# Strip input rows at a stride of 576 elements, split weights 128 bytes further on, a smaller dynamic scratch

## The chip, the cores and the metric

The kernel runs on one core of one Trainium2 chip. The metric is the device time of one execution in microseconds. Engines are called PE (TensorE; PEld is its weight load), ACT (ScalarE), DVE (VectorE), POOL (GpSimd) and SP (SyncE, which issues DMAs).

## What is computed

Two transformer layers in a row on 512 tokens of width 1024, in float32, each behind 16 meta tokens, so that 528 positions are worked on. The first layer merges three branches (a chunkwise retention, a differential attention, a short convolution) and has an MLP of 4096 with a squared ReLU. The second merges a stick-breaking attention and a gated linear attention and has a gated MLP of 2816 with a short convolution. Nearly all arithmetic is in the products of activations with weight matrices:

```python
(rq, rk, rv, rg, dq, dk, dv, cb, cc, cx, gates) = [h @ w_in[:, s:e] for s, e in column_bounds()]
merged = g0 * (ret @ w_branch[0]) + g1 * (diff @ w_branch[1]) + g2 * (conv @ w_branch[2])
x = x + merged @ w_out
x = x + jnp.square(jax.nn.relu(rms_norm(x, norm2_w) @ w_up)) @ w_down
# second layer
proj = hn @ w_in_2
mix = (gate_sb * (sb @ w_sb_out) + gate_gla * (o @ w_gla_out)) @ w_o
ffn = (gelu(causal_dwconv(hn @ w_ffn_up)) * (hn @ w_ffn_gate)) @ w_ffn_down
```

## The kernel before

Activations lie feature-major: a buffer `[128, 8, 528]` has feature 128 c + p in row c of partition p, and 528 columns, one for each position (T = 528, HALF = 264, NM = 16, SEQ = 512). A weight matrix is cut into strips of 128 output features: `[128, 8, 128]`, eight blocks of 128 by 128, 512 bytes each in a partition.

*Three products for one.* Products are made in the format fp32r, from a high and a low part of each operand. `xh` and `xl` (or `bh` and `bl`) hold the parts of the activations, `wh` and `wl` those of the weights, and a strip is wh x hi + wh x lo + wl x hi, added up in PSUM.

*The pipeline of a strip.* SP loads strip n into `wraw` (two slots, 512 KB each, line 466). ACT copies it to `wh` (`split_hi`, from line 548, the copy is line 553), DVE subtracts to get `wl` (`split_lo`, the subtraction is line 1231), PE multiplies (`strip`, from line 2150, its matmul is line 2171), DVE or ACT reads PSUM. ACT may split strip n + 1 only when PE is through with strip n - 1 (`mm_done`). There are 299 such loads by SP.

*The order within a strip.* As a rule a strip is three passes: all eight rows with wh and hi, all eight with wh and lo, all eight with wl and hi. If all 528 positions are wanted, a row is two matmuls of 264 columns, one after the other, with the same weights (16 in a pass); if only the 512 tokens are, it is one of 512 columns that begins at column 16 (8 in a pass). A strip whose input rows are still being made (`ready` is given) goes row by row in place of that: the three products of row 0, then those of row 1, and so on. Every matmul has its own load of weights.

*Other users of these buffers.* Line 2770 (`chunk_products`) makes the down product of the second MLP with tokens as output partitions: there 512 columns of wh or wl are the moving operand and 128 columns of a bh or bl row, from column 16 + 128 t on, the stationary one. Line 2294 (`st_product`) makes blocks of 256 tokens with additions of sub-blocks in place of some multiplications, from xh, xl and other buffers. In the stick-breaking attention, which needs only four rows of xh and xl, the upper four (`sb_hi`, `sum_hi`) serve as flat scratch. POOL loads the 12 tables of decays and slopes into `hf` one head ahead (line 2877), the only transfers whose descriptors software makes.

*Placement.* Buffers are laid out in the order in which they are allocated, behind the scratch for dynamic transfers (16384 bytes in a partition) and 128 bytes of constants: xh, xl, bh, bl, wraw, wh, wl, then all the others.

Of the kernel before, what the change touches and what calls it, by code (L numbers as in the profile page):

```python
# [21 lines left out]
F32R = mybir.dt.float32r  # L22
# [5 lines left out]
P = 128  # L28
D = 1024
KC = D // P  # L30
NM = 16
SEQ = 512
T = NM + SEQ
# [4 lines left out]
DH, DHD = 8, 64  # L38
LAM_INIT = 0.2
FF1 = 4 * D  # L40

SH, SHD = 8, 64
GH, GDV = 4, 256
# [37 lines left out]
def flat(ap):  # L81
    return ap.rearrange("p a t -> p (a t)")
# [35 lines left out]
def build(nc, weights, cols, tables, consts, lam_rows, post_rows, x_t, meta2_t, wgk, gla_masks, res_dram,  # L118
          mrg_dram, tx_dram, out):
    ctx = ExitStack()  # L120
    with ctx:
        def sb(name, shape, dt=F32):
            return ctx.enter_context(nc.sbuf_tensor(name, shape, dt))
# [4 lines left out]
        def shared(name, shape):  # L128

            with nc.sbuf_tensor(name, shape, F32) as plain:  # L130
                pass
            return plain, sb(name + "_r", shape, F32R)


        xh, xl = sb("xh", [P, KC, T], F32R), sb("xl", [P, KC, T], F32R)
        bh, bl = sb("bh", [P, KC, T], F32R), sb("bl", [P, KC, T], F32R)

        wraw = sb("wraw", [P, 2, KC, P])
        wh, wl = sb("wh", [P, 2, KC, P], F32R), sb("wl", [P, 2, KC, P], F32R)
        qq, qqr = shared("qq", [P, KC, T])  # L140
        kk, kkr = shared("kk", [P, KC, T])
        vt, vtr = shared("vt", [P, 5, D])
# [44 lines left out]
        SBW = SBA + SBB + SBC  # L187
# [3 lines left out]
        sbr = [flat(kkr)[:, SBW * e:SBW * e + SBW] for e in range(2)]  # L191
        SBZ = 272 + 400 + 400
        sums = [[flat(r)[:, SBZ * e:SBZ * e + SBZ] for e in range(2)] for r in (xrows, xrowsr)]
        sb_hi = [flat(r[:, 4:8, :])[:, 0:SBW] for r in (xh, xl)]
        sum_hi = [flat(r[:, 4:8, :])[:, SBW:SBW + 672] for r in (xh, xl)]
        sum2_hi = [gater[:, 144 * e:144 * e + 144] for e in range(2)]
        ntri_r, nones_r = hfr[:, 1, 0:P], hfr[:, 1, P:2 * P]
        sb_v = tmp[:, 0, :]
# [2856 lines left out]
```

How the kernel before makes its waits and increments, by code:

```python
    def __call__(self, ins):  # L91
        ins.then_inc(self.sem, 1)
        self.n += 1
        self.eng.wait_ge(self.sem, self.base + self.n)
# [368 lines left out]
        @block.sync  # L463
# [5 lines left out]
            def strip_pairs(first, end):  # L469
                if first < end:
                    with sp.Fori(first, end) as i:
                        for k in range(2):
                            sp.wait_ge(lo_done, 2 * i + k - 1)
                            load(2 * i + k, k)
# [9 lines left out]
                    sp.dma_start(st_area(q)[:, 2 * k:2 * k + 2, :].rearrange("p b n -> p (b n)"),  # L484
                                 weights[n0 + k].rearrange("p k n -> p (k n)")).then_inc(st_in[q % 2][k], 16)
            gates = gate_pairs()
            strip_pairs(1, 9)
            load_area(*gates[0])
            strip_pairs(9, 12)
            for m, (q, n0) in enumerate(gates):
                if m + 1 < CONV_PAIRS:
                    sp.wait_ge(*((lo_done, n0 - 2) if m else (t_made, 4)))
                    load_area(*gates[m + 1])
                for k in range(2):
                    sp.wait_ge(lo_done, n0 - 1 + k)
                    load(n0 + 2 + k, k)
            gates = gate_pairs("ret")
            strip_pairs(START["ret_qkv"] // 2, gates[0][1] // 2)
            sp.wait_ge(op_ready, 2 * KC)
            for m, (q, n0) in enumerate(gates):
                if m == 0:
                    load_area(*gates[0])
# [118 lines left out]
            def st_copy(q, src, dst, product, k):  # L623
                act.wait_ge(st_mm, 5 * q + product)
                if k == 0:
```

## Time and profile before

| | |
|---|---|
| median of 3 runs | 2125.64 us (2125.48 to 2125.77) |
| the profiled execution, first to last instruction | 2123.7 us |
| PE busy | 2111.8 us (99%), 13662 matmuls |
| PEld busy | 1859.1 us (88%) |
| DVE busy | 1241.8 us (58%) |
| ACT busy | 831.0 us (39%) |
| POOL busy | 165.7 us (8%) |
| DMA, mean over the span | 96 GB/s |

The profile gives no own run time of the profiled execution; its span is 1.9 us below the median. Busy time counts overlapping matmuls once. The duration of one matmul is from its start to its modelled end, and successive ones overlap; the time from one start to the next is called its pace here.

### The profile page before, as it was taken

The numbers are of one execution on the slowest core, as the hardware profiler recorded it, in microseconds if no ns is written. First come the engines' busy times: TensorE is split into PE (matmuls) and PEld (weight loads), VectorE is DVE, ScalarE is ACT, GpSimd is POOL, SyncE is SP. The second block draws the span as 40 slices with busy tenths as digits, with TensorE's granted clock in tenths as the row PEclk, the third lists the DMA queues.
The fourth block names the chain that finished last, engine by engine and source line by source line (L and its number), as shares of the span: only waits on it lengthen the run. The fifth ranks groups of instructions, "written<-read, shape, count | busy, mean of one in ns | idle before, by whom it ended". The sixth has DMA issues, their size and how long they took to land.

```text
span 2123.7 us, 33898 instructions
## 1 busy us (share of the span) xinstructions
PE 2111.8 (99%) x13662; PEld 1859.1 (88%) x13662; DVE 1241.8 (58%) x1847; ACT 831.0 (39%) x1305; POOL 165.7 (8%) x146
## 2 busy tenths in 40 slices
PE   9999999999999999999999999999999999999998
PEld 8998888788888788898898888999999998889897
DVE  6674444564555555767664666367855567446364
ACT  4333222433444443434434566343424344222233
POOL 0012000030000000232120000022300000000000
PEclk9999999999999999999999999999999999999999
DMA  4343221522222323332322221231133222322322
GB/s 149 109 171 107 85 75 60 198 81 82 73 68 68 106 94 98 107 109 80 109 90 90 88 91 50 90 121 54 58 136 106 90 79 90 99 90 89 99 90 99
DMA packets 53563, 203.36 MB, mean 96 GB/s; under 512 B 6960, under 2 KB 7344, under 8 KB 52288
## 3 DMA queue, kind: packets, MB, share of 16 engines
q1 hardware_dynamic: 49248, 177.56, 26.1%
q10 hardware_dynamic: 3232, 20.80, 2.5%
q0 software_dynamic: 960, 3.24, 0.5%
q8 instruction: 91, 1.49, 0.3%
q14 instruction: 32, 0.26, 0.0%
HBM read 190.96 MB, written 10.62 MB: 95 GB/s over the span
## 4 chain that ended last, share of the span: by engine, by line
PE 94%; DVE 3%; ACT 2%; issue 0%; DMA 0%; DVEq 0%; SPq 0%; ACTq 0%
PE ps L2171 70%; PE ps L2294 7%; PE ps L2770 6%; PE ps L2636 1%; PE ps L2418 1%; PE ps L2443 1%; PE ps L2371 1%; PE ps L2702 1%; PE ps L2542 1%; DVE kk_r L1824 1%; PE ps L2457 1%; ACT kk L963 1%; ACT kk L964 1%; PE ps L2680 0%; PE ps L2523 0%; PE ps L2350 0%
## 5 line engine op out<-in xcount | busy, mean ns | idle before, releaser
L553 ACT ACTIVATE wh<-wraw 128x1024 fp32r<-128x1024 f32 x284 | 300.0, 1056 | 747.6 <-PE ps L2171 632.1
L1231 DVE TENSOR_TENSOR wl<-wraw,wh 128x1024 fp32r<-128x1024 f32 x298 | 366.9, 1232 | 135.8 <-ACT wh L553 131.7
L2171 PE MATMUL ps<-xh,wh 128*128 128x264 f32 (+1 forms) x1800 | 327.6, 327 | 0.5 <-DVE tmp L1264 0.4
L2171 PE MATMUL ps<-xl,wh 128*128 128x264 f32 (+1 forms) x1800 | 321.3, 324 | 0.0
L2171 PE MATMUL ps<-xh,wl 128*128 128x264 f32 (+1 forms) x1800 | 320.8, 323 | 0.0
L2171 PEld LDWEIGHTS ps<-xh,wh 128*128 128x128 f32 x1800 | 264.7, 188 | 31.6 <-issue 2.4
L2171 PEld LDWEIGHTS ps<-xl,wh 128*128 128x128 f32 x1800 | 266.2, 188 | 28.6
L2171 PEld LDWEIGHTS ps<-xh,wl 128*128 128x128 f32 x1800 | 266.1, 188 | 28.4
L2171 PE MATMUL ps<-bh,wh 128*128 128x264 f32 (+1 forms) x1296 | 234.4, 325 | 0.2 <-ACT wh L553 0.2
L2171 PE MATMUL ps<-bl,wh 128*128 128x264 f32 (+1 forms) x1296 | 231.0, 322 | 0.0
L2171 PE MATMUL ps<-bh,wl 128*128 128x264 f32 (+1 forms) x1296 | 230.6, 322 | 0.0
L2171 PEld LDWEIGHTS ps<-bh,wh 128*128 128x128 f32 x1296 | 190.9, 188 | 21.7 <-issue 1.5
L2171 PEld LDWEIGHTS ps<-bl,wh 128*128 128x128 f32 x1296 | 191.3, 188 | 19.8 <-issue 0.2
L2171 PEld LDWEIGHTS ps<-bh,wl 128*128 128x128 f32 x1296 | 191.0, 188 | 19.6
L1264 DVE TENSOR_TENSOR qq<-ps,rsq 128x528 f32<-128x528 f32 (+1 forms) x44 | 30.8, 700 | 98.3 <-PE ps L2171 98.2
L1264 DVE TENSOR_TENSOR tmp<-ps,rsq 128x528 f32<-128x528 f32 x31 | 21.9, 707 | 81.2 <-PE ps L2171 79.2
L561 ACT ACTIVATE bh<-hf 128x512 fp32r<-128x512 f32 (+1 forms) x30 | 19.0, 632 | 88.4 <-DVE hf L2079 51.4
L2770 PE MATMUL ps<-wh,bh 128*128 128x512 f32 x176 | 50.1, 393 | 0.3 <-ACT ps L1199 0.3
L2770 PE MATMUL ps<-wh,bl 128*128 128x512 f32 x176 | 50.0, 393 | 0.0
L2770 PE MATMUL ps<-wl,bh 128*128 128x512 f32 x176 | 50.0, 393 | 0.0
L2917 POOL TENSOR_TENSOR qq<-qq,kk 128x512 f32<-128x512 f32 x3 | 5.0, 1663 | 571.8 <-DVE qq L2139 571.8
L1724 DVE SCALAR_TENSOR_TENSOR hf<-ps,rsq 128x512 f32<-128x512 f32 x32 | 22.1, 689 | 38.2 <-PE ps L2171 38.2
(532 smaller groups left out, 2779.6 us busy)
## 6 DMA issues: line engine op xcount, KB each, us to landing
wraw<-weights_dram SPq DMA_DIRECT2D x299, 512.0 KB, 3.5
qq<-weights_dram SPq DMA_DIRECT2D x12, 512.0 KB, 4.1
kk<-weights_dram SPq DMA_DIRECT2D x12, 512.0 KB, 4.4
hf<-tables_dram POOLq DMA_DIRECT2D x12, 264.0 KB, 3.0
res<-x_t_dram SPq DMA_DIRECT2D x4, 528.0 KB, 7.1
res<-x_t_dram ACTq DMA_DIRECT2D x1, 2112.0 KB, 9.2
res_dram<-res ACTq DMA_DIRECT2D x1, 2112.0 KB, 6.4
mrg_dram<-mrg ACTq DMA_DIRECT2D x1, 2112.0 KB, 9.0
```

What stands on the lines that cost most here:

```text
L553: nc.scalar.activation(wh[:, slot], wraw[:, slot], ACT.Copy).then_inc(hi_done, 1)
L963: link(nc.scalar.activation(sbt[e], sbt[e], ACT.Exp, scale=-1.0))
L964: nc.scalar.activation(sbt[e], sbt[e], ACT.Ln, bias=1.0).then_inc(slog_done, 1)
L1231: nc.vector.tensor_tensor(wl[:, slot], wraw[:, slot], wh[:, slot].bitcast(F32), ALU.subtract)\
L1264: return nc.vector.tensor_tensor(dst, src, row(rsq, n), ALU.mult)
L1724: nc.vector.scalar_tensor_tensor(out=hf[:, j, NM:T], in0=slot_ap(p0[2], SEQ), scalar=0.0, in1=rsq[:, NM:T], op0=ALU.max, op1=ALU.mult)\
L1824: ins = nc.vector.tensor_tensor(dst, src, hi.bitcast(F32), ALU.subtract)
L2171: last = nc.tensor.matmul(o, w[:, slot, c, :], a[:, c, tok], start=(k == 0), stop=(k == len(steps) - 1))
L2294: last = nc.tensor.matmul(st_bank(bank), w[:, c, :], a(c), start=(first and c == 0 and w is w_hi and a is acts[0]), stop=(c == 3 and w is ...
L2371: nc.tensor.matmul(ps[:, 5 + v, q0:SEQ], vt[:, t, f:f + P], at[:, t, q0:SEQ], start=(t == 0), stop=False)
L2418: ins = nc.tensor.matmul(ps[:, 2 + m, off:off + W], dq[h % 2][f, NM + P * b:NM + P * b + P], dk[h % 2][f, 0:W], start=True, stop=True)
L2770: last = nc.tensor.matmul(ps[:, 2 * t + h, :], a[:, c, NM + P * t:NM + P * t + P], w[:, slot, 4 * h:4 * h + 4, :].rearrange("p k n -> p (k ...
```

## The change

The four strip input buffers get rows of 576 elements, of which 528 are used: `xh` and the others become views of the first 528 columns, and the matmuls, copies and subtractions name the same elements as before. The flat scratch in the upper four rows is taken from the whole rows. A spare buffer of 32 elements (128 bytes) stands ahead of `wh` and another behind `wl`. The scratch for dynamic transfers goes from its default of 16384 bytes to 4096. No instruction is added, removed or moved.

```diff
--- before.py
+++ after.py
@@ -38,6 +38,7 @@
 DH, DHD = 8, 64
 LAM_INIT = 0.2
 FF1 = 4 * D
+ROW = 576
 
 SH, SHD = 8, 64
 GH, GDV = 4, 256
@@ -132,11 +133,13 @@
             return plain, sb(name + "_r", shape, F32R)
 
 
-        xh, xl = sb("xh", [P, KC, T], F32R), sb("xl", [P, KC, T], F32R)
-        bh, bl = sb("bh", [P, KC, T], F32R), sb("bl", [P, KC, T], F32R)
+        x_rows, b_rows = ([sb(n + part, [P, KC, ROW], F32R) for part in "hl"] for n in "xb")
+        (xh, xl), (bh, bl) = ([r[:, :, 0:T] for r in two_of] for two_of in (x_rows, b_rows))
 
         wraw = sb("wraw", [P, 2, KC, P])
+        sb("ahead_of_weights", [P, 32])
         wh, wl = sb("wh", [P, 2, KC, P], F32R), sb("wl", [P, 2, KC, P], F32R)
+        sb("behind_weights", [P, 32])
         qq, qqr = shared("qq", [P, KC, T])
         kk, kkr = shared("kk", [P, KC, T])
         vt, vtr = shared("vt", [P, 5, D])
@@ -191,8 +194,8 @@
         sbr = [flat(kkr)[:, SBW * e:SBW * e + SBW] for e in range(2)]
         SBZ = 272 + 400 + 400
         sums = [[flat(r)[:, SBZ * e:SBZ * e + SBZ] for e in range(2)] for r in (xrows, xrowsr)]
-        sb_hi = [flat(r[:, 4:8, :])[:, 0:SBW] for r in (xh, xl)]
-        sum_hi = [flat(r[:, 4:8, :])[:, SBW:SBW + 672] for r in (xh, xl)]
+        sb_hi = [flat(r[:, 4:8, :])[:, 0:SBW] for r in x_rows]
+        sum_hi = [flat(r[:, 4:8, :])[:, SBW:SBW + 672] for r in x_rows]
         sum2_hi = [gater[:, 144 * e:144 * e + 144] for e in range(2)]
         ntri_r, nones_r = hfr[:, 1, 0:P], hfr[:, 1, P:2 * P]
         sb_v = tmp[:, 0, :]
@@ -3042,7 +3045,7 @@
     from concourse.bass_utils import run_bass_kernel_spmd
 
     arrays = device_inputs({k: np.asarray(v) for k, v in inputs.items()})
-    nc = bacc.Bacc("TRN2", target_bir_lowering=False, num_devices=1)
+    nc = bacc.Bacc("TRN2", target_bir_lowering=False, num_devices=1, dynamic_dma_scratch_size=4096)
     args = {n: nc.dram_tensor(f"{n}_dram", v.shape, F32, kind="ExternalInput").ap() for n, v in arrays.items()}
     res_dram = nc.dram_tensor("res_dram", [P, KC, T], F32).ap()
     mrg_dram = nc.dram_tensor("mrg_dram", [P, KC, T], F32).ap()
```

## Rows read from the trace of the kernel before

**Rows 1.** The page: busy us, share and instructions by engine; granted clock in 40 slices
```profile
PE 2111.8 (99%) x13662; PEld 1859.1 (88%) x13662; DVE 1241.8 (58%) x1847; ACT 831.0 (39%) x1305; POOL 165.7 (8%) x146
...
PEclk9999999999999999999999999999999999999999
```

**Rows 2.** PE's waits, the longest: us in total, times, longest us
```profile
PE ps L2277 <- DVE kk L1267: 1.5, 1, 1.5
```

**Rows 3.** Groups by form on PE: count | busy us, mean ns of one | idle before
```profile
L2171 PE MATMUL ps<-xl,wh 128*128 128x512 f32 x648 | 169.2, 394 | 0.0
...
L2171 PE MATMUL ps<-xl,wh 128*128 128x264 f32 x1152 | 152.1, 284 | 0.0
...
L2171 PE MATMUL ps<-bl,wh 128*128 128x512 f32 x448 | 117.4, 394 | 0.0
...
L2171 PE MATMUL ps<-bl,wh 128*128 128x264 f32 x848 | 113.6, 284 | 0.0
...
L2770 PE MATMUL ps<-wh,bl 128*128 128x512 f32 x176 | 50.0, 393 | 0.0
...
L2294 PE MATMUL ps<-xl,wh 128*128 128x256 f32 x100 | 15.9, 281 | 0.0
```

**Rows 4.** PE in order of time, four passes: start us, us, line, operation, count
```profile
1181.07 2.01 PE L2171 MATMUL ps<-xl,wh 128*128 128x512 f32 x8
...
1184.78 1.55 PE L2171 MATMUL ps<-xh,wh 128*128 128x512 f32 x6
...
2064.93 2.10 PE L2171 MATMUL ps<-xh,wl 128*128 128x264 f32 x16
...
2066.86 0.40 PE L2171 MATMUL ps<-xh,wh 128*128 128x512 f32 x1
```

**Rows 5.** Line 2171, windows under 0.1 us: duration ns min/median/max, first and last start
```profile
L2171 PE MATMUL ps<-xh,wl x2: 282/284/285, 2064.9 to 2065.1; 128*128 128x264 f32 x2
...
L2171 PE MATMUL ps<-xh,wl x2: 278/280/283, 2065.4 to 2065.5; 128*128 128x264 f32 x2
...
L2171 PE MATMUL ps<-xh,wl x2: 288/288/288, 2065.7 to 2065.8; 128*128 128x264 f32 x2
...
L2171 PE MATMUL ps<-xl,wh x1: 393/393/393, 1181.5 to 1181.5; 128*128 128x512 f32 x1
```

**Rows 6.** Line 2770 in order of time (start us, us); last, its whole first run
```profile
1849.08 1.08 PE L2770 MATMUL ps<-wl,bh 128*128 128x512 f32 x4
...
1850.91 1.08 PE L2770 MATMUL ps<-wh,bl 128*128 128x512 f32 x4
...
1855.48 1.07 PE L2770 MATMUL ps<-wh,bh 128*128 128x512 f32 x4
...
1857.29 1.07 PE L2770 MATMUL ps<-wl,bh 128*128 128x512 f32 x4
...
1858.20 1.09 PE L2770 MATMUL ps<-wh,bh 128*128 128x512 f32 x4
...
1860.07 1.09 PE L2770 MATMUL ps<-wl,bh 128*128 128x512 f32 x4
...
1836.24 44.26 PE ps L2770 x192
```

**Rows 7.** The page, ACT's splits: count | busy us, mean ns | idle before, releaser
```profile
L553 ACT ACTIVATE wh<-wraw 128x1024 fp32r<-128x1024 f32 x284 | 300.0, 1056 | 747.6 <-PE ps L2171 632.1
```

**Rows 8.** The page, table loads: KB each, median us from issue to landing
```profile
hf<-tables_dram POOLq DMA_DIRECT2D x12, 264.0 KB, 3.0
```

**Rows 9.** PE in order of time, a strip taken row by row, rows 2 and 6
```profile
1640.40 0.41 PE L2171 MATMUL ps<-xh,wh 128*128 128x264 f32 x2
...
1641.14 0.41 PE L2171 MATMUL ps<-xh,wh 128*128 128x264 f32 x2
...
1643.32 0.41 PE L2171 MATMUL ps<-xh,wh 128*128 128x264 f32 x2
...
1644.07 0.41 PE L2171 MATMUL ps<-xh,wh 128*128 128x264 f32 x2
```

## The prediction

> **What bounds the kernel now.** I read the page's shares first, then who PE waits for, then the groups of matmuls by form, then single passes in order of time. PE is busy 99% of the span at the full granted clock, 1.00 in every stretch, so the level is 2.4 GHz throughout [rows 1]. Its longest wait is 1.5 us, once [rows 2]; span less busy time leaves 2123.7 - 2111.8 = 11.9 us. The end is therefore set by how fast matmuls follow one another, and almost all of them are of two forms: the moving operand is a piece of a strip input row (xh, xl, bh, bl), 264 or 512 columns wide, and the stationary one a block of a split strip (wh, wl). Line 2171 has 3 x (1152 + 848) = 6000 of the first form and 3 x (648 + 448) = 3288 of the second [rows 3]. Line 2770, the token-major down product, has 3 x 176 = 528 with the roles turned: wh and wl move, rows of bh and bl are stationary.
>
> **The pace of one matmul.** A pass of 16 matmuls of 264 columns starts at 2064.93 and the next at 2066.86: 1930 / 16 = 120.6 ns each. Sixteen of 512 columns take from 1181.07 to 1184.78: 3710 / 16 = 231.9 ns [rows 4]. At one column per tick of 2.4 GHz these would be 110.0 and 213.3 ns, so 10.6 and 18.6 ns of each is something else, without a gap or a wait: 6000 x 10.6 + 3288 x 18.6 = 125 us of the span. That is what there is to win.
>
> **Does it hang on addresses?** The buffers lie one after another behind the dynamic scratch. Before: 16384 bytes of scratch and 128 of constants, then xh at 16512, which is 128 over a multiple of 256. The four row buffers (16896 bytes, 66 x 256 each) and wraw, wh and wl (8192 each) keep that, so all start at 128 (mod 256). Row c of a strip input starts c x 2112 bytes on, which is 64c (mod 256); its second half is 1056 bytes on, 32 (mod 256). Rows 0 to 3 thus start at 128, 192, 0 and 64, and 4 to 7 repeat it, while a weight block always starts at 128.
>
> The durations follow just that cycle. In one and the same pass row 0's halves last 285 and 282 ns. Row 2's last 278 and 283, row 3's 288 both [rows 5]. Over whole forms the mean is 284, and 394 for 512 columns [rows 3]. I read one ns of duration as one ns of pace: a matmul lasts longer than its pace by 284 - 120.6 = 163.4 ns in the one form and 394 - 231.9 = 162.1 in the other, a tail that the next one overlaps and that hardly differs.
>
> Line 2770 shows that the weights' place counts too. There the moving operand always starts at 128 (mod 256) and the stationary one at 192 + 64c (columns from 16 on of row c). Eight matmuls with the stationary one at 64 (c = 2) take 1.83 us, from 1849.08 to 1850.91: 228.8 ns each. At 128 (c = 3) eight take 1.81 us from 1855.48 to 1857.29: 226.3. At 192 (c = 4) eight take 1.87 us from 1858.20 to 1860.07: 233.8. All of line 2770 has 44.26 us for 192, 230.5 [rows 6].
>
> **The change, part by part.**
> *Addresses.* After: 4096 + 128 puts xh at 4224, again 128 (mod 256). A row is now 2304 bytes, 9 x 256, so every row starts at 128, its second half at 160, and the 512-column piece (from column 16) at 192. The 128 spare bytes put wh and wl at 0; the 128 behind them put everything later back to 128. No instruction is added or removed, and no wait.
> *264 columns.* Start 128 or 160 with weights at 0: moving operand and weights are 128 bytes apart. Today's row 2 has that distance (0 or 32 against 128), and is the fastest: (278 + 283) / 2 = 280.5 against 284, -3.5 ns [rows 5]. 6000 x 3.5 = -21.0 us. Bounds: every one as the single best, 278, is -6 ns, -36 us; for the other end see the second rival, +18 us. I take row 2's pair, the only one with the same distance in the same order of passes.
> *512 columns.* 192 against 0 is the distance of row 2 here too (64 against 128): 393 [rows 5] against 394, -1 ns, x 3288 = -3.3 us. Bounds: line 2770's fastest pace, 226.3 against 231.9, is -5.6 ns or -18 us; its slowest, 233.8, is +1.9 ns or +6.2 us.
> *Line 2770.* Now wh and wl move from 0 and the stationary block is always at 192: distance as with 128 against 64 today, 228.8 against 230.5, -1.7 x 528 = -0.9 us; between -2.2 us (at 226.3) and +1.7 us (at 233.8).
> *The rest of PE.* Line 2294's 300 matmuls with an xh or xl row and some others (400 and 448 columns) get new distances; their 281 ns lies between all these values [rows 3], so 0, with +-1.5 us for a few ns each.
> *ACT and DVE.* The splits write to other addresses in rows of the same length. Both are off the path: ACT sits idle 632.1 us before its splits, waiting for PE to be done with a slot [rows 7]. If a split's 1056 ns became 1200, this would hide it; 0 us. If PE gets faster by 3.5 ns in 120.6, a strip of some 5.6 us shrinks by 0.16 us, against that idle time, so nothing is late next.
> *Dynamic scratch.* It can only concern the 12 table loads from POOL, 3.0 us each from issue to landing, issued one head ahead by the code [rows 8]. Cost 0. Were each to wait for the one before, 12 x 3.0 = 36 us would be added to loads for which PE has no wait over 1.5 us, and the distance between heads hides them. It can't give a gain.
>
> **The sum.** -21.0 - 3.3 - 0.9 = -25.2 us. The profiled execution has a span of 2123.7 us, and the median of the runs is 2125.64, 1.9 us around it. On the span that is 2098.5, and as a run 2125.64 - 25.2 = 2100.4.
>
> **Rivals.**
> *Pace is columns alone.* The 10.6 and 18.6 ns are then a fixed rate of reading four-byte columns, and the cycle of 278 to 288 ns only shifts time between neighbours in a contiguous stream, with a sum that stays. For it: over four rows the durations even out at 284. Against it: line 2770's paces differ for eight matmuls on end, over the same columns [rows 6]. Time 2125.6, within 0.2%. This is also what a page says: the Trainium skill ("TensorE: Matmul & The Clock Gate", Back-to-back issue gap) gives an isolated gap of N/2.4 + 2.5 ns, with no address in it. For 264 and 512 columns that would be 112.5 and 215.8 ns, and the trace's 120.6 and 231.9 disagree.
> *A steady distance costs more than a changing one.* Row 2 is fast where row 1 stands ahead of it. In the strips that wait for their rows one by one, the three products of one row follow each other, so that the distance stays for six matmuls (wh with xh and xl, wl with xh, two halves each). Row 2 then takes 0.74 us for six (1640.40 to 1641.14) and row 6 0.75 us (1643.32 to 1644.07) [rows 9]: 124 ns by these rows, 123 at the low end of their rounding. I take 3 above 120.6, where the forecast counts on 3.5 below. After the change the distance never changes but for the halves. Then 6000 x 3 = +18 us, and the 512-column form, whose distance of 64 bytes (weights ahead) is line 2770's slow one, adds 1.9 x 3288 = +6.2 us: 2150. For it: line 2770's matmuls are steady as well. Against: the six include repeats of the same weights, which a pass hasn't, and within them single pairs are mixed. With the 512 columns at their slow value (+6.2) and line 2770's -0.9, it decides from a 264-column pace of 120.6 - 5.3 / 6 = 119.7 ns on: above that the change loses.
> *A floor.* Fixed distances let the pair settle at the best values seen, 278 ns and 226.3: -36 - 18 = -54 us, 2072.
>
> **How the numbers follow.** The forecast 0.40, the floor or most of the way to it 0.10, no effect 0.14, the steady loss 0.36. The likeliest case's own range is 2090 to 2112. The whole range goes two thirds of the way from the forecast to the floor, and up nearly to the loss: 2082 to 2147 leaves some 0.1 on each side. Measurement can tell 0.2%, 4.3 us, from no change. Chances: faster 0.50, within 0.14, slower 0.36.
>
> **What the changed profile would show.** If right: all durations of one form alike in a pass (280 and 281 ns, no cycle over four rows), a 264-column pass of 1.87 us in place of 1.93, 512 columns at 231, line 2770 at 44.0 us or less for 192, idle of PE still near 12 us. Wrong on the first rival: durations alike at 284. Wrong on the second: 264-column passes of 1.96 us and more. A wait of PE for hf or for wh that grows would speak against what I costed at nothing.

## The result

| | before | changed |
|---|---|---|
| median | 2125.56 us (2125.48 to 2125.77, 4 runs) | 2139.44 us (2138.67 to 2140.18, 4 runs) |
| profiled execution, span | 2123.7 us | 2138.4 us |
| PE busy | 2111.8 us | 2126.1 us |

The changed kernel takes 1.0065 times as long (95% interval 1.0053 to 1.0077), 13.9 us more. The forecast was 2100.4: the wrong side. The runs of the changed kernel lie in two pairs, 1.4 us apart, and its profile is of the slower pair.

The profile after, page first, the lines that answer to [rows 1], [rows 7] and [rows 8]:

```profile
PE 2126.1 (99%) x13662; PEld 1869.1 (87%) x13662; DVE 1238.6 (58%) x1847; ACT 831.1 (39%) x1305; POOL 164.3 (8%) x146
...
PEclk9999999999999999999999999999999999999999
...
L556 ACT ACTIVATE wh<-wraw 128x1024 fp32r<-128x1024 f32 x284 | 300.0, 1056 | 759.3 <-PE ps L2174 645.5
...
hf<-tables_dram POOLq DMA_DIRECT2D x12, 264.0 KB, 3.0
```

PE is busy for 14.3 of the 14.7 us that the span grew, at the same granted clock, with the same 13662 matmuls. Its idle time is 12.3 us, before 11.9. ACT's split lasts the same 1056 ns and waits a little longer for PE; the table loads land after the same 3.0 us. So the time came in inside the matmuls. Their groups by form (count | busy us, mean ns of one | idle before), against [rows 3]:

```profile
L2174 PE MATMUL ps<-xl,wh 128*128 128x512 f32 x648 | 170.3, 395 | 0.0
...
L2174 PE MATMUL ps<-xl,wh 128*128 128x264 f32 x1152 | 154.2, 286 | 0.0
...
L2174 PE MATMUL ps<-bl,wh 128*128 128x512 f32 x448 | 118.1, 395 | 0.0
...
L2174 PE MATMUL ps<-bl,wh 128*128 128x264 f32 x848 | 115.2, 286 | 0.0
...
L2297 PE MATMUL ps<-xl,wh 128*128 128x256 f32 x100 | 15.6, 278 | 0.0
```

For line 2174 that is 286 in place of 284, and 395 in place of 394: 6000 x 2 + 3288 x 1 = 15.3 us, about the growth. In order of time (start us, us, line, operation, count), passes that answer to [rows 4], and one whole run of the down product that answers to the last of [rows 6]:

```profile
1188.14 2.03 PE L2174 MATMUL ps<-xl,wh 128*128 128x512 f32 x8
...
1191.87 2.03 PE L2174 MATMUL ps<-xh,wh 128*128 128x512 f32 x8
...
2079.26 2.12 PE L2174 MATMUL ps<-xh,wl 128*128 128x264 f32 x16
2081.22 1.09 PE L2174 MATMUL ps<-xh,wh 128*128 128x512 f32 x4
...
1849.99 43.96 PE ps L2773 x192
```

A pass of 264 columns takes 1.96 us (122.5 ns each, before 120.6). Sixteen matmuls of 512 columns take 3.73 us (233.1, before 231.9). Line 2770, here 2773, is faster: 43.96 us for 192 against 44.26. So are two of the three groups of line 2294 that read xh or xl, here line 2297 (278 ns on the mean, before 281). Line 2171 is line 2174 here.

### The profile page after: what moved, and what is told of

It is laid out like the page before. It is cut to its first block, busy times and chain, and to the rows that moved or that the text cites. A ratio compares the mean times of both kernels' runs of the same rounds, so it can differ in the third digit from the quotient of the medians.

```text
span 2138.4 us, 33898 instructions
## 1 busy us (share of the span) xinstructions
PE 2126.1 (99%) x13662; PEld 1869.1 (87%) x13662; DVE 1238.6 (58%) x1847; ACT 831.1 (39%) x1305; POOL 164.3 (8%) x146
## 4 chain that ended last, share of the span: by engine, by line
PE 94%; DVE 3%; ACT 2%; issue 0%; DMA 0%; DVEq 0%; SPq 0%; ACTq 0%
PE ps L2174 70%; PE ps L2297 7%; PE ps L2773 5%; PE ps L2639 1%; PE ps L2421 1%; PE ps L2446 1%; PE ps L2374 1%; PE ps L2705 1%; PE ps L2545 1%; DVE kk_r L1827 1%; PE ps L2460 1%; ACT kk L966 1%; ACT kk L967 1%; PE ps L2683 0%; PE ps L2526 0%; PE ps L2353 0%
## 5 line engine op out<-in xcount | busy, mean ns | idle before, releaser
L556 ACT ACTIVATE wh<-wraw 128x1024 fp32r<-128x1024 f32 x284 | 300.0, 1056 | 759.3 <-PE ps L2174 645.5
L1234 DVE TENSOR_TENSOR wl<-wraw,wh 128x1024 fp32r<-128x1024 f32 x298 | 367.0, 1233 | 135.0 <-ACT wh L556 131.1
L2174 PE MATMUL ps<-bh,wl 128*128 128x264 f32 (+1 forms) x1296 | 233.4, 324 | 0.0
L2174 PE MATMUL ps<-bl,wh 128*128 128x264 f32 (+1 forms) x1296 | 233.3, 324 | 0.0
```

The costliest lines, as they stand in the source:

```text
L556: nc.scalar.activation(wh[:, slot], wraw[:, slot], ACT.Copy).then_inc(hi_done, 1)
L1234: nc.vector.tensor_tensor(wl[:, slot], wraw[:, slot], wh[:, slot].bitcast(F32), ALU.subtract)\
L2174: last = nc.tensor.matmul(o, w[:, slot, c, :], a[:, c, tok], start=(k == 0), stop=(k == len(steps) - 1))
```

## The experiments

Starting places are given mod 256. *Distance* is the start of the moving operand less the start of the weight block, mod 256. In the kernel before it is 64c + 0 or + 32 for the two 264-column halves of row c, and 64c + 64 for 512 columns. In the changed kernel it is 128 and 160 for every row, and 192 for 512 columns.

Line 2770 has its roles turned: its moving operand is wh or wl and its weight block, the stationary one, a piece of a bh or bl row, so its distance is 192 - 64c before and 64 for every row in the changed kernel.

Three theories stood at the outset. **A**: with a fixed distance, that distance sets the pace. **B**: a stride under which the distance never changes costs by itself. **C**: the smaller scratch costs. From e5 on **D** stood against A: what counts is the place of the weights alone.

### e1 to e4: one part at a time, and the weights elsewhere

e1, the row stride without the shift of the weights:

```diff
-        sb("ahead_of_weights", [P, 32])
-        sb("behind_weights", [P, 32])
+        sb("behind_weights", [P, 64])
```

> The row stride of 576 as in the change, but wh and wl stay at 128 (mod 256); all 256 spare bytes stand behind wl. Theory A, the distance (moving start minus weight start, mod 256) in a steady state sets the pace: 264 columns stand at 0 and 32, where the kernel before, in strips taken row by row, needs 0.72 us for six in rows 0 and 4, 120.3 ns; 512 columns at 64, where line 2770 before needs 228.8 ns. Against 120.9 and 231.8 that is -4 and -10 us: 2112 (2108 to 2118). Rival B, a stride without a change of phase costs by itself, whatever the distance: as slow as the changed kernel, 2139 or more, with 264 columns over 122.5 and 512 at 233. Rival C, the smaller scratch costs: 2139 too.

Measured: 2117.08 us, ratio 0.996 (0.9946 to 0.9974). The stride alone makes the kernel 8.4 us *faster*, so B falls, and C with it, as the small scratch is in e1 too.

```profile
2045.08 2.08 PE L2173 MATMUL ps<-xh,wl 128*128 128x264 f32 x16
2047.00 2.01 PE L2173 MATMUL ps<-xh,wh 128*128 128x512 f32 x8
2048.85 2.00 PE L2173 MATMUL ps<-xl,wh 128*128 128x512 f32 x8
2050.68 1.99 PE L2173 MATMUL ps<-xh,wl 128*128 128x512 f32 x8
...
1827.57 44.79 PE ps L2772 x192
```

These are passes of e1 in order of time, then its first run of line 2770. The 264-column pass is down to 1.92 us, the 512-column one to 1.83 (228.8 ns: distance 64, to the tenth what line 2770 took before at 64). Line 2770 itself, whose distance is now 192, goes up to 44.79 us, 233.3 ns. The expected 2112 had left that out; it gives back 2.75 x 0.53 = 1.5 us. The rest of the 5 us to 2112 lies in the 512 columns: of the 255 second and third passes of eight, 209 are at 228.8 ns but 46 at 233.3, 229.9 over the whole trace (from the matmul records), so that they gave 6 us and not 10.

e2, the shift of the weights without the stride (`ROW = 528` in the changed kernel):

> The spare bytes and the small scratch as in the change, but rows 528 elements apart: the distances still run through all four values (two for each row), only from another row on. A: the mean over the cycle stays, 2125.6 (2123 to 2128), and the cycle of durations (278 to 288 ns) moves by two rows, so that the fastest pair is rows 0 and 4. B: also 2125.6, since phases change. If the shift of the weights by itself is what costs: 2139. C, the scratch costs: 2139.

Measured: 2125.36 us, ratio 0.9999 (0.999 to 1.0009), as both said. What the run is worth lies in its durations. Row 0 of e2 has the addresses (mod 256) of every row of the changed kernel: moving at 128 and 160, weights at 0. Two windows under 0.1 us (ns min/median/max), the first of e2's row 0, the second of row 1 in a 264-column pass of the changed kernel:

```profile
L2174 PE MATMUL ps<-xh,wl x2: 278/280/283, 2064.9 to 2065.0; 128*128 128x264 f32 x2
```

```profile
L2174 PE MATMUL ps<-xh,wl x2: 286/288/290, 2079.5 to 2079.6; 128*128 128x264 f32 x2
```

The same addresses, 278 and 283 ns where the row before has other ones, 290 and 286 where it has the same. By the records the row before it in that pass has 282 and 283 and the row behind it 284 and 286, and then the three repeat: the changed kernel has a cycle too, but none of its three pairs is as quick as e2's.

e3, the kernel before with the scratch of 4096 bytes alone:

> The kernel before with a dynamic scratch of 4096 bytes, all buffers 12288 bytes lower (48 x 256, so no address changes mod 256). A and B: 2125.6, within 1 us, table loads at 3.0 us. C: up to 2139, with longer or later table loads.

Measured: 2125.48 us, ratio 1.0 (0.999 to 1.001), table loads at 3.0 us. C falls by itself too.

e4, the changed kernel with the weights 64 bytes on from where they were before, in place of 128:

```diff
-        sb("ahead_of_weights", [P, 32])
+        sb("ahead_of_weights", [P, 16])
-        sb("behind_weights", [P, 32])
+        sb("behind_weights", [P, 48])
```

> Rows of 576, wh and wl at 192 (mod 256), 64 bytes further than before. A: 512 columns stand at distance 0, line 2770's fastest (226.3 to 227 ns, -4.8 x 3312 = -16 us); 264 columns at 192 and 224, where strips taken row by row before need 0.73 us for six, 122 ns (+1.1 x 6672 = +7 us); line 2770 at distance 0, -3.5 x 528 = -2 us. Sum -11: 2115 (2109 to 2121). B: 2139 or more, like the changed kernel.

Measured: 2102.32 us, ratio 0.9891 (0.9874 to 0.9907), faster than both kernels. Passes of e4, and its first run of line 2770:

```profile
2031.24 2.08 PE L2174 MATMUL ps<-xh,wl 128*128 128x264 f32 x16
2033.16 2.01 PE L2174 MATMUL ps<-xh,wh 128*128 128x512 f32 x8
2035.01 1.98 PE L2174 MATMUL ps<-xl,wh 128*128 128x512 f32 x8
2036.82 1.98 PE L2174 MATMUL ps<-xh,wl 128*128 128x512 f32 x8
2038.63 2.09 PE L2174 MATMUL ps<-xh,wh 128*128 128x264 f32 x16
...
1816.80 43.52 PE ps L2773 x192
```

The 512-column passes behind the first take 1.81 us, 226.3 ns, which is what line 2770 took at distance 0 before. The 264-column pass takes 1.92 us, 120.0 ns, where I had expected 122 from the strips taken row by row. That difference, 2 x 6672 = 13 us, is why the time fell below the expected 2109 to 2121.

### e5 to e8: is it the distance, and how fine?

The same two lines again, with 48, 8 and 24 elements ahead of the weights (16, 56 and 40 behind, so that it is 64 in all).

> Rows of 576, wh and wl at 64 (mod 256). Theory A, the steady distance sets the pace: 512 columns at distance 128, 232.1 ns as line 2770 before has it there (+1 us); 264 columns at 64 and 96, untried steadily, between the 120.2 found at distance 0 and the 122.9 at 128: 121.5 (+4 us); line 2770 at 128, 232.1 (+1 us). 2131 (2126 to 2137). Rival D, the absolute place of the weights counts and not the distance: a time that falls steadily from w = 0 (2139) over 64 and 128 (2117) to 192 (2102), thus near 2128; it gives no higher pace for 512 columns here than at w = 128 plus 1.7 ns.

Measured: 2135.34 us, ratio 1.0046 (1.0026 to 1.0065). A's 2131 with its range holds; D's falling line would have given some 2128.

> Rows of 576, wh and wl at 160, between e1 (128) and e4 (192): 264 columns at 224 and 0, 512 at 32. A, if the pace is smooth in the distance: 264 at 120.1 (-5 us), 512 at 228.5 (-11 us), line 2770 at 224, 230 (0): 2110. If only whole steps of 64 bytes count, the time is that of e1 (2117) or of e4 (2102).

Measured: 2125.63 us, ratio 1.0 (0.9989 to 1.0011). The 264 columns came out as expected, but 32 bytes off distance 0 the gain for 512 columns is gone altogether. Passes of e6:

```profile
2055.25 2.03 PE L2174 MATMUL ps<-xh,wh 128*128 128x512 f32 x8
2057.12 2.03 PE L2174 MATMUL ps<-xl,wh 128*128 128x512 f32 x8
2058.98 2.03 PE L2174 MATMUL ps<-xh,wl 128*128 128x512 f32 x8
2060.85 2.08 PE L2174 MATMUL ps<-xh,wh 128*128 128x264 f32 x16
```

1.865 us, 233 ns, against 1.81 in e4. The pace is not smooth in the distance, and my halfway value of 228.5 was wrong.

> Rows of 576, wh and wl at 224, between e4 (192) and the changed kernel (0): 264 columns at 160 and 192, 512 at 224. A, smooth: 264 at 121.5 (+4 us), 512 at 230.3 (-5 us), line 2770 at 32, 228.5 (-1 us): 2124 (2115 to 2130). If only whole steps of 64 bytes count: 2102 or 2139.

Measured: 2126.1 us, ratio 1.0003 (0.9992 to 1.0014). It lies in the stated range by luck: 512 columns were at 233.2 ns where I had 230.3 and line 2770 at 233.3 where I had 228.5, as in e6, and 264 columns at 120.2 where I had 121.5, and the errors cancel. The paces are the evidence here, not the total.

e8 moves the row buffers and the weights together:

```diff
+        sb("ahead_of_rows", [P, 16])
         x_rows, b_rows = ([sb(n + part, [P, KC, ROW], F32R) for part in "hl"] for n in "xb")
...
+        sb("behind_rows", [P, 48])
         wraw = sb("wraw", [P, 2, KC, P])
```

> The rows of xh, xl, bh and bl moved 64 bytes on as well as the weights of e4, 64 bytes on: rows at 192, weights at 0 (mod 256), the distances of e4 with the weights' place of the changed kernel. A, distance alone: 2102, with 264 columns at 120.1 and 512 at 227.2. D, absolute place of the weights: near the changed kernel, 2139, with 122.9 and 233.3.

Measured: 2105.03 us, ratio 0.9903 (0.9875 to 0.9932). The weights lie where they lie in the changed kernel, and the time is 34 us shorter. D falls. The groups by form are those of e4, 282 for 264 columns and 389 for 512, and line 2770 has its 43.52 us too:

```profile
L2176 PE MATMUL ps<-bl,wh 128*128 128x512 f32 x448 | 115.2, 389 | 0.0
...
L2176 PE MATMUL ps<-bl,wh 128*128 128x264 f32 x848 | 112.6, 282 | 0.0
...
1819.59 43.52 PE ps L2775 x192
```

The 2.7 us to e4 are line 2294's, some of whose operands stayed where they were: over its 1332 steps under 200 ns, start to start is 119.4 ns on the mean in e8 and 117.2 in e4, 2.9 us.

All paces at a fixed distance, as means over the whole trace of start-to-start times of matmuls of one form on end (worked out from every matmul record, without steps over 250 ns for 512 columns and 140 ns for 264; the kernel before in the last column, with its changing distance):

| distance | 0 | 32 | 64 | 128 | 160 | 192 | 224 | before |
|---|---|---|---|---|---|---|---|---|
| 512 columns, strips, ns | 227.4 (e4) | 233.3 (e6) | 229.9 (e1) | 232.8 (e5) | | 233.3 (changed) | 233.2 (e7) | 231.8 |
| 512 columns, line 2770, ns | 226.8 (e4) | 233.3 (e7) | 229.8 (changed) | 233.2 (e5) | | 233.3 (e1) | 233.3 (e6) | 230.7 |
| 264 columns, first half there, ns | 120.3 (e1) | | 122.0 (e5) | 122.8 (changed) | 120.2 (e7) | 120.1 (e4) | 120.2 (e6) | 120.9 |

The first two rows come from different runs and from different places of both operands, and agree to within 0.6 ns at every distance. That, with e8, is what speaks for the distance and against the place of either operand alone.

A mean can hide more than one pace. In the changed kernel 148 of the 244 second and third passes of 264 columns run at 123.3 ns, 90 at 122.2 and 6 at 120.0. These 6 belong to three strips, 30 us apart, here the first, right behind a matmul of line 2558 (its three passes, then its second pass in ns min/median/max):

```profile
1271.00 2.08 PE L2174 MATMUL ps<-bh,wh 128*128 128x264 f32 x16
1272.92 2.08 PE L2174 MATMUL ps<-bl,wh 128*128 128x264 f32 x16
1274.84 2.08 PE L2174 MATMUL ps<-bh,wl 128*128 128x264 f32 x16
...
L2174 PE MATMUL ps<-bl,wh x16: 280/282/283, 1272.9 to 1274.7; 128*128 128x264 f32 x16
```

They take 1.92 us at the distances at which the others take 1.96 or 1.97. So the mean over the trace goes with the distance, but the distance does not by itself fix the pace of every strip.

### e9 and e10: within one strip, and a distance that alternates

e9 is e4 with `wl` 64 bytes further than `wh`:

```diff
-        wh, wl = sb("wh", [P, 2, KC, P], F32R), sb("wl", [P, 2, KC, P], F32R)
+        wh = sb("wh", [P, 2, KC, P], F32R)
+        sb("between_weights", [P, 16])
+        wl = sb("wl", [P, 2, KC, P], F32R)
```

> As e4 (rows of 576, wh at 192), but wl 64 bytes further, at 0 (mod 256). The third pass of a strip (wl with hi) then has the changed kernel's distances, the first two keep those of e4. A, the distance of the two operands of a matmul sets its pace: the third pass at 233.3 and 122.9 ns, the others at 227.2 and 120.1; 1104 x 6.1 + 2224 x 2.8 = +13 us, some more in line 2770 for its third: 2116 (2112 to 2120). If the pace hung on where ACT and DVE read and write while PE works, or on the strip as a whole, all three passes would change alike.

Measured: 2120.46 us, ratio 0.9976 (0.9965 to 0.9987). Passes of e9:

```profile
2046.70 2.08 PE L2176 MATMUL ps<-xl,wh 128*128 128x264 f32 x16
2048.62 2.13 PE L2176 MATMUL ps<-xh,wl 128*128 128x264 f32 x16
2050.59 2.01 PE L2176 MATMUL ps<-xh,wh 128*128 128x512 f32 x8
2052.44 1.98 PE L2176 MATMUL ps<-xl,wh 128*128 128x512 f32 x8
2054.25 2.03 PE L2176 MATMUL ps<-xh,wl 128*128 128x512 f32 x8
2056.12 2.09 PE L2176 MATMUL ps<-xh,wh 128*128 128x264 f32 x16
```

The second passes keep e4's 1.92 and 1.81 us. The third, with wl, take 1.97 and 1.87, near the changed kernel's values. So the slow pace goes with the matmuls whose own two operands stand at the slow distance, not with the strip as a whole. Nor is it what ACT and DVE do meanwhile: by the records, steps in third passes of 512 columns during which both are mostly idle have 233.3 ns in the changed kernel and 226.7 in e4, and those with DVE alone busy have 233.4 and 226.7. The total is 18 us over e4 where I had 13, just above the stated 2112 to 2120; line 2770 (231.2 ns, in e4 226.8) has 2.3 us of it. Over the trace, the first passes of 512-column strips (wh with hi) have a median pace of 230.8 ns in e9 and 226.7 in e4, at the same distance. It looks as if a slow pass were still felt in the first pass behind it; no run tests that.

e10 is e4 with `ROW = 544`:

> As e4, but rows 544 elements apart (2176 bytes, 8.5 x 256): distances alternate from row to row, 264 columns between 192 and 64, 512 between 0 and 128. If a changing distance costs the mean of the steady paces: 264 at (120.1 + 122.0) / 2 = 121.1 (+1 us), 512 at (227.2 + 232.9) / 2 = 230.1 (-6 us), line 2770 alike (-1 us): 2120 (2115 to 2126). If change itself is cheap, as row 2's 280.5 ns in passes of the kernel before suggested: below 2115. If change itself costs: over 2126.

Measured: 2126.17 us, ratio 1.0002 (0.9991 to 1.0014), just above the stated 2115 to 2126. Groups of e10 by form:

```profile
L2174 PE MATMUL ps<-xl,wh 128*128 128x512 f32 x648 | 168.2, 392 | 0.0
...
L2174 PE MATMUL ps<-xl,wh 128*128 128x264 f32 x1152 | 153.9, 286 | 0.0
```

512 columns came out at the mean of their two steady paces (230.1 by all records, as expected). 264 columns did not: 122.1 ns where both steady paces lie at or below 122.0 and their mean is 121.1; that is 1.0 x 6672 = 7 us, about the whole gap to 2120. So a change of distance costs something here for 264 columns, and nothing in the kernel before, whose 120.9 ns lie below the mean of the four steady paces, 121.3.

## Why the prediction was wrong

**The bound: right.** PE's matmuls, their two forms and their pace set the end. The experiments moved by what those paces give.

**That addresses matter: right, and the first rival is out.** "Pace is columns alone" is ruled out by e4 and e8 against the changed kernel: the same columns, 34 to 37 us apart. The isolated gap that the Trainium skill gives ("TensorE: Matmul & The Clock Gate", Back-to-back issue gap), with no address in it, fails here in the same way: at 512 columns it is 215.8 ns, and the runs have 226.8 to 233.3 on the mean.

**"264 columns" is the step that failed.** I took row 2's 278 and 283 ns as what every row would get at row 2's distance, -3.5 ns, -21.0 us. Measured: +1.9 ns by pass (1.96 us for 16 in place of 1.93) and +2 by form, 6000 x 2 = +12 us. Of the 39 us between forecast and result, 33 are in this step. The value was no property of the distance: row 2 was quick where row 1 stood ahead of it, as e2 shows at the addresses (mod 256) of the changed kernel. The counterpart stood in the same [rows 5], row 3's 288 ns: over the second and third passes of the kernel before, rows 0 to 3 have paces of 120.6, 121.1, 117.8 and 124.1 ns, so row 3 gives back what row 2 gains. At a fixed distance row 3's is among the quickest (120.1, e4) and row 2's is the slowest (122.8). Even the three strips of the changed kernel that do have durations of 280 and 283 ns have a pace of 120.0, not the forecast 117.1. (There a duration exceeds the pace by 161.5 ns, not 163.4, so one ns of duration is only roughly one of pace.) The trace of before had the better row, and I gave it to the second rival with less weight: at a distance that stays, rows 2 and 6 took 0.74 and 0.75 us for six [rows 9]. From the kernel's records their mean is 123.3 ns, and the changed kernel has 122.8.

**"512 columns" failed the same way, in the small.** From row 2's 393 ns I had -3.3 us. At a fixed distance of 192 the pace is 233.3, what line 2770 had with the weights 64 bytes ahead (233.8 by two rows), so +1.5 x 3288 = +5 us, 8 us beyond what I had; with the 33 that is 41, and line 2294 gives most of the surplus back. It had stood in that step as the upper bound.

**Line 2770: right.** 43.96 us against "44.0 us or less"; its two operands kept one distance for 24 matmuls on end before too, so the value carried over. By all records it went from 230.7 to 229.8 ns, -0.5 us where the sum has -0.9.

**The second rival** had the mechanism and the sign. Its price, +24 us and 2150, was too high by 11 us: for 264 columns it took 3 ns, from two rows of 0.01 us resolution, where 2 are found; for 512 columns its +6.2 us is close to the +5 found.

**The sum, from the records:** 6000 x 1.92 = +11.5 us (264 columns), +4.9 (512 columns), -0.5 (line 2770), and for line 2294, costed at 0 with +-1.5, 119.0 ns down to 118.1, -1.2. That is 14.7 us, the growth of the span.

**At nothing: right.** ACT and DVE (durations 1056 and 1233 ns, before 1056 and 1232), scratch (e3), idle time of PE (12.3 us).

**The range** held the time only because it was stretched over the other case; the changed profile's marks of the second rival ("264-column passes of 1.96 us and more") came true to the digit.

## What to carry to other kernels

Where PE is busy throughout and matmuls take longer than their columns at the granted clock, look at where the moving operand and the weight block start. A uniform stride is worth having only together with the right distance: the same 576-element rows gave +0.65%, +0.46%, -0.4% and -1.1% with the weights 128, 192, 0 and 64 bytes on.

A duration from a repeating pattern belongs to the pattern. Before scaling one up to a state in which nothing changes from one instruction to the next, look for a place in the trace where nothing changes already; here the down product had the values to within some 1 ns, and the strips taken row by row had them to within 0.5 ns at distances 0, 64 and 128, but 2 ns too high at 192 (122.2 against 120.1, the miss of e4). Add up the whole cycle as well: a quick member can be paid for by its neighbour.

## What the runs showed of the hardware

- The pace of fp32r matmuls of 512 columns goes with the distance mod 256 of their two operands in the partition: on the mean 226.8 to 227.4 ns at 0, 229.8 to 229.9 at 64, 232.8 to 233.3 at 32, 128, 192 and 224. Moving both operands by 64 bytes changes nothing in the strips (e8).
- For 512 columns, 32 bytes off the best place cost as much as 128 (e6, e7). For 264 columns in two halves only 64 and 128 are slower (122.0 and 122.8 ns); the other four lie at 120.1 to 120.3.
- At one and the same fixed distance there are several patterns. In the changed kernel one pass has durations from 282 to 290 ns, in a cycle of three rows:

```profile
L2174 PE MATMUL ps<-xh,wl x3: 282/283/290, 2079.3 to 2079.5; 128*128 128x264 f32 x3
```

  By the records, other passes there alternate between 286 and 288, and those of three strips between 280 and 283. What picks the pattern stays open, and so does what inside the chip makes the distance count; only the addresses were varied.
